# First expert product of a diffusion-transformer layer: sharing one 512-column matmul between the two halves of the activations

## The reference

```
q = (h @ w_q).reshape(B, T, PEER_HEADS, 2, PEER_DHALF)
s = einsum('bshid,hikd->bshik', q, sub_keys)
s1, i1 = top_k(s[..., 0, :], 16); s2, i2 = top_k(s[..., 1, :], 16)
top_s, pos = top_k(s1[..., :, None] + s2[..., None, :], 16)   # of the 256 sums
g = softmax(top_s)
act = gelu(einsum('cd,ced->ce', h, u[idx]))
out = einsum('ce,ced->cd', g * act, v[idx])
```

## Time and profile before

| | |
|---|---|
| median of three runs | 2128.35 us (2126.1 to 2129.22) |
| the profiled execution | 2125.87 us |
| its span, first to last instruction | 2124.1 us |
| mean granted TensorE clock | 0.993 |
| busy: PE, DVE, ACT, POOL | 2075.6, 1657.9, 1231.0, 312.1 us |
| HBM traffic | 247 GB/s over the span |

### The profile page before, as it was taken

The page is one execution under the profiler, slowest core; times in us unless marked ns, Lnnn a source line. Parts: engine busy times, 40 slices in busy tenths (PEclk is TensorE's granted clock), DMA queues, the critical chain, the costliest instruction groups (busy, mean ns, idle before and its releaser), DMA issues.

```text
span 2124.1 us, 41214 instructions
## 1 busy us (share of the span) xinstructions
PE 2075.6 (98%) x13458; PEld 1842.5 (87%) x13458; DVE 1657.9 (78%) x2947; ACT 1231.0 (58%) x2273; POOL 312.1 (15%) x264
## 2 busy tenths in 40 slices
PE   6999999999999999999999999999999999999997
PEld 3568888668999999999999999999878888888886
DVE  3467777897775688888787688888688989989997
ACT  3332225686444677777766655555566666666666
POOL 0000000000000000000000211111344555323320
PEclk9999999999999999999999999999999999999999
DMA  9968887401765455555598644445789999999992
GB/s 366 408 246 300 284 282 264 159 1 51 263 246 184 155 177 184 182 182 178 181 360 309 203 157 156 159 157 182 263 297 365 371 352 358 344 360 354 395 352 95
DMA packets 160917, 524.86 MB, mean 247 GB/s; under 512 B 34976, under 2 KB 35792, under 8 KB 160208
## 3 DMA queue, kind: packets, MB, share of 16 engines
q1 hardware_dynamic: 123840, 452.63, 59.2%
q0 software_dynamic: 20576, 67.20, 9.1%
q10 hardware_dynamic: 16432, 4.19, 0.9%
HBM read 515.52 MB, written 8.39 MB: 247 GB/s over the span
## 4 chain that ended last, share of the span: by engine, by line
PE 90%; DVE 4%; DMA 2%; ACT 2%; issue 1%; SPq 0%; POOL 0%; DVEq 0%; ACTq 0%
PE PS L890 73%; PE PS L1287 10%; PE PS L1228 2%; PE PS L946 1%; DVE st L1535 1%; DMA ada_t<-w_ada 1%; PE PS L1073 1%; DVE w_lo L1335 1%; PE PS L878 1%; PE PS L897 1%; ACT pr L634 0%; DVE mixed L1908 0%; PE PS L1061 0%; DMA x_c<-x_ctx 0%; DMA raw<-stream 0%
## 5 line engine op out<-in xcount | busy, mean ns | idle before, releaser
L475 ACT ACTIVATE w_hi<-raw 128x512 fp32r<-128x512 f32 x1088 | 682.2, 630 | 687.5 <-PE PS L890 527.5
L1335 DVE TENSOR_TENSOR w_lo<-raw,w_hi 128x512 fp32r<-128x512 f32 x1088 | 731.5, 690 | 331.0 <-ACT w_hi L475 305.2
L890 PE MATMUL PS<-h_h,w_hi 128*128 128x256 f32 (+1 forms) x2304 | 658.0, 286 | 1.6 <-ACT A L739 1.0
L890 PE MATMUL PS<-h_l,w_hi 128*128 128x256 f32 (+1 forms) x2304 | 652.8, 283 | 0.0
L890 PE MATMUL PS<-h_h,w_lo 128*128 128x256 f32 (+1 forms) x2304 | 652.8, 283 | 0.0
L890 PEld LDWEIGHTS PS<-h_h,w_hi 128*128 128x128 f32 x2304 | 443.1, 192 | 2.7 <-ACT A L739 1.2
L890 PEld LDWEIGHTS PS<-h_l,w_hi 128*128 128x128 f32 x2304 | 443.2, 192 | 0.0
L890 PEld LDWEIGHTS PS<-h_h,w_lo 128*128 128x128 f32 x2304 | 443.0, 192 | 0.0
L890 PE MATMUL PS<-w_hi,p_hl 128*128 128x512 f32 x1024 | 399.5, 390 | 6.4 <-issue 4.7
L890 PEld LDWEIGHTS PS<-w_hi,p_hl 128*128 128x128 f32 x1024 | 192.2, 188 | 50.5 <-issue 8.5
L890 PE MATMUL PS<-w_lo,p_hl 128*128 128x512 f32 x512 | 199.3, 389 | 0.0
(11 more groups left out here) (253 smaller groups left out, 2836.2 us busy)
## 6 DMA issues: line engine op xcount, KB each, us to landing
raw<-stream SPq DMA_DIRECT2D x544, 512.0 KB
raw_far<-stream SPq DMA_DIRECT2D x104, 512.0 KB
ada<-w_ada SPq DMA_DIRECT2D x96, 512.0 KB, 4.6
ada_t<-w_ada SPq DMA_DIRECT2D x64, 512.0 KB, 9.7
ada_u<-w_ada SPq DMA_DIRECT2D x32, 512.0 KB, 5.9
values_scratch<-A ACTq DMA_DIRECT2D x1, 2560.0 KB, 19.0
x_c<-x_ctx SPq DMA_DIRECT2D x1, 2048.0 KB, 7.8
x<-x_lat SPq DMA_DIRECT2D x1, 2048.0 KB, 15.2
```

What stands on the lines that cost most here:

```text
L475: nc.scalar.activation(w_hi[:, (2 * j + hf) % SPLIT, :], ring[:, j, hf * HALF:(hf + 1) * HALF], ACT.Copy).then_inc(S["w_high"], 1)
L890: ins = mm(out_, l_, r_, start=(start and q == 0), stop=(stop and q == 2), skip_group_check=check)
L1335: V_.tensor_tensor(w_lo[:, h % SPLIT, :], ring[:, h // 2 % RAW, at_:at_ + HALF], w_hi[:, h % SPLIT, :].bitcast(F32), ALU.subtract).then_in ...
```

## The change

In tiles 0 to 59, `h2_h` and `h2_l` become one tensor `h2`, and a block's products with `w_hi` are one matmul of 512 columns: `w_hi x h2_h` lands in the left half of the bank and `w_hi x h2_l` in the right. The product `w_lo x h2_h` is added to the left half. ScalarE copies the right half to SBUF (`keep_side`, into `rstd`, free by then), VectorE adds the left half to it (`sum_sides`), and gelu reads the sum from SBUF. TensorE waits for that sum (`sides_summed`) before it enters a bank again. A small gelu before each of ScalarE's loops loads the gelu table, under which Copy works too. The stretch before the gates grows by one turn (`GATES_AT` 30), with five halves in place of four at eight places of the one-hot steps. Three of POOL's six memsets move ahead of the wait for the one-column products. Tiles from 60 on are as before.

```diff
-        h2_h = at("h2_h", [P, KT, T], F32R, R + 128 * KB)
-        h2_l = at("h2_l", [P, KT, T], F32R, R + 144 * KB)
+        h2 = at("h2", [P, 2, KT, T], F32R, R + 128 * KB)
+        h2_h, h2_l = h2[:, 0], h2[:, 1]
...
+            for i in (80, 96, 104):
+                tiles_of_ones(i)
             pool.wait_ge(S["ada_col"], 8)
-            for i in range(2 * ROUTE_AT, NE_TILES, 8):
-                nc.gpsimd.memset(A[:, i:i + 8, :], 1.0).then_inc(S["tiles_one"], 1)
+            for i in (88, 112, 120):
+                tiles_of_ones(i)
...
+            def gelu_summed(i):
+                act.wait_ge(S["sides_summed"], i + 3)
+                nc.scalar.activation(A[:, bass.ds(i, 1), :].rearrange("p a t -> p (a t)"), rstd[:],
+                                     ACT.Gelu_apprx_tanh).then_inc(S["gelu_done"], 1)
+            def keep_side(i, bank):
+                act.wait_ge(S["w_free"], 4 * i + (2 * U_U + 4 + SPLIT))
+                act.wait_ge(S["gelu_done"], i + 2)
+                nc.scalar.activation(rstd[:], PS[:, bank, T:2 * T], ACT.Copy).then_inc(S["side_kept"], 1)
...
-            u_tiles(0, GATES_AT)
+            def summed_turn(b, first=False):
+                for i in range(2):
+                    split_high(b + (34 + i), (2, 0)[i])
+                    act.wait_ge(raw_in[(3, 1)[i]], 16 * b + 16 * (34 + i) + 16)
+                    half_high(b + (34 + i), (3, 1)[i], 0)
+                    if not (first and i == 0):
+                        gelu_summed(2 * b + (i - 1))
+                    keep_side(2 * b + i, i)
+                    half_high(b + (34 + i), (3, 1)[i], 1)
...
+            nc.scalar.activation(modc[:, 30:31], eps[:], ACT.Gelu_apprx_tanh)
+            summed_tiles(GATES_AT)
             act.wait_ge(S["top_s_ready"], 1)
             nc.scalar.activation(ge[:], tops[:], ACT.Exp).then_inc(S["top_exp"], 1)
+            nc.scalar.activation(modc[:, 31:32], eps[:], ACT.Gelu_apprx_tanh)
             u_tiles(GATES_AT, ROUTE_AT - GATES_AT)
...
+            def summed_product(n):
+                with pe.Fori(0, n) as b:
+                    for h in range(8):
+                        i = h // 4
+                        pe.wait_ge(S["w_low"], 8 * b + (2 * U_U + h + 1))
+                        if h % 4 == 0:
+                            pe.wait_ge(S["sides_summed"], 2 * b + (i + 1))
+                        for q in range(4):
+                            k = 4 * (h % 4) + q
+                            cols = slice(q * P, (q + 1) * P)
+                            mm(PS[:, i, :], w_hi[:, h % SPLIT, cols], h2[:, :, k, :], start=(k == 0), stop=False,
+                               skip_group_check=True)
+                            ins = mm(PS[:, i, 0:T], w_lo[:, h % SPLIT, cols], h2_h[:, k, :], start=False,
+                                     stop=(k == KT - 1), skip_group_check=True)
+                        used(ins)
...
-            first_product(0, LATE_ADA_AT + 8, False)
+            summed_product(GATES_AT)
+            first_product(GATES_AT, LATE_ADA_AT + 8 - GATES_AT, False)
...
+            def sum_sides(i):
+                dve.wait_ge(S["side_kept"], i + 1)
+                V_.tensor_tensor(rstd[:], PS[:, i % 2, 0:T], rstd[:], ALU.add).then_inc(S["sides_summed"], 1)
             half = [2 * (U_U + 2)]
             def next_low(n):
                 for _ in range(n):
+                    tile, part = divmod(half[0] - 2 * U_U, 4)
+                    if part == 3 and tile <= 2 * GATES_AT:
+                        sum_sides(tile - 1)
                     half_low(half[0] // 8, half[0] % 8)
                     half[0] += 1
...
-GATES_AT = 29
+GATES_AT = 30
```

More of the change, by code:

```diff
@@ L106, in block_program @@
                      "top_s_ready top_exp gates_ready gates_turned gates_kept gelu_done gelu_in tiles_one "
-                     "dist_b dist_b2 hot_a hot_b routed route_used p_high p_high_too p_low picks_ready picks_in far_ready values_kept mixed y_kept_a y_kept_d y_turned x3_ready x3_scaled sq_summed").split()
+                     "side_kept sides_summed dist_b dist_b2 hot_a hot_b routed route_used p_high p_high_too p_low picks_ready picks_in far_ready values_kept mixed y_kept_a y_kept_d y_turned x3_ready x3_scaled sq_summed").split()
         S = {n: ctx.enter_context(nc.semaphore(n)) for n in sem_names}
@@ L422, in _, with tiles_of_ones @@
                 nc.gpsimd.dma_start(dst[0:PICKED], near[PICKED:P, a, :]).then_inc(S["picks_in"], 16)
+            def tiles_of_ones(i):
+                nc.gpsimd.memset(A[:, i:i + 8, :], 1.0).then_inc(S["tiles_one"], 1)
+            for i in (80, 96, 104):
+                tiles_of_ones(i)
             pool.wait_ge(S["ada_col"], 8)
-            for i in range(2 * ROUTE_AT, NE_TILES, 8):
-                nc.gpsimd.memset(A[:, i:i + 8, :], 1.0).then_inc(S["tiles_one"], 1)
+            for i in (88, 112, 120):
+                tiles_of_ones(i)
             pool.wait_ge(S["gates_kept"], 6)
@@ L763, in u_tiles, with summed_tiles @@
                     gelu(2 * b + 1, 1)
-            u_tiles(0, GATES_AT)
+            def summed_turn(b, first=False):
[7 more added lines that the diff above has]
+                    half_high(b + (34 + i), (3, 1)[i], 1)
+            def summed_tiles(n):
+                summed_turn(0, first=True)
+                with act.Fori(1, n) as b:
+                    summed_turn(b)
+                gelu_summed(2 * n - 1)
+            nc.scalar.activation(modc[:, 30:31], eps[:], ACT.Gelu_apprx_tanh)
+            summed_tiles(GATES_AT)
             act.wait_ge(S["top_s_ready"], 1)
             nc.scalar.activation(ge[:], tops[:], ACT.Exp).then_inc(S["top_exp"], 1)
+            nc.scalar.activation(modc[:, 31:32], eps[:], ACT.Gelu_apprx_tanh)
             u_tiles(GATES_AT, ROUTE_AT - GATES_AT)
@@ L1247, in _ @@
             pe.sem_inc(S["gelu_done"], 2)
+            pe.sem_inc(S["sides_summed"], 2)
             pe.sem_inc(S["routed"], 2)
-            first_product(0, LATE_ADA_AT + 8, False)
+            summed_product(GATES_AT)
+            first_product(GATES_AT, LATE_ADA_AT + 8 - GATES_AT, False)
             ada_columns(6, 6, acc_u)
@@ L1780, in _ @@
                                           iota16[:].unsqueeze(1).broadcast_to([P, P, 16]), ALU.is_equal))
-                    next_low(4)
+                    next_low(5)
                     hv = hit[:].rearrange("p (h k) a -> p h k a", h=HEADS)
```

## The result

The changed kernel takes 2113.43 us (median of 7 runs, 2109.66 to 2122.25), the kernel before 2128.35 (7 runs, 2126.1 to 2131.59): ratio 0.9935, 95% interval 0.9919 to 0.9952. Twelve more runs of the same text beside 25 of the kernel before gave 2117.66 against 2127.43: ratio 0.995, 0.9934 to 0.9966. The forecast was 2116.0.

What follows compares the result with a forecast made beforehand. TensorE's matmul pitch was taken as the bound: 12.5 us saved by merged matmuls, less 0.5 at the stretch's end, gives -12.0 us, from 2128.35 to 2116.3, stated as 2116.0 us; own range 2112.5 to 2118.5, wider range 2112 to 2122.

Steps and rivals of the forecast that it cites:

- The term of 12.5 us: TensorE, tiles 0 to 59: one fixed part of 0.0130 us less per block, 60 tiles x 16 blocks, 12.5 us off.
- The forecast of 12.0: Whole kernel: 12.5 us gained in the matmuls less 0.5 lost at the end of the stretch, 12.0 us faster.
- Rival A: 512-column matmul loses its gain through its two-piece operand beside a 256; 0.2396 us or more a pair, 2129 us; chance 0.07.
- a pair above 0.35: Tiles 0 to 59: a pair step above 0.35 us would show the forecast wrong and Rival A right.
- The 333.5 us for the tiles: Sign that the forecast is right: TensorE's 60 tiles in the stretch take about 333.5 us, where they took 346.3.
- VectorE keeps up: Tiles 0 to 59: with the addition VectorE keeps up in each of three search rhythms, at 85 to 94%.
- Rival B: VectorE late at 28 wide search steps, 0.1 to 0.3 us each; 3 to 8 us, 2119 to 2124; chance 0.12.
- C's point of 0.8 us: VectorE becomes the bound if an addition with its exposed wait costs over 0.8 us; 2138 us at 1.2; chance 0.05.
- This saves nothing by itself: ScalarE, tiles 0 to 59: work falls from 4.2 to 3.3 us per tile, but TensorE never waited for it.
- case D: Table loads stay; ScalarE needs 4.6 of 5.54 us a tile and still isn't waited for; 2116 to 2118; chance 0.02.
- End of the stretch: Before the gates, TensorE's wait of 1.0 us grows as w_lo's come later; cost 0.3 to 0.6 us, 0.5 taken.

## Why the prediction was right

**The pitch.** The term of 12.5 us was 960 times the fixed part of a matmul, 13 ns, from the earlier trace rows. Measured: 0.3600 us for three of 256 (apart), 0.3467 for the pair in its fast rhythm, 13.3 ns x 960 = 12.8 us. With the fixed part of about 2.5 ns that the Trainium skill gives (TensorE: Matmul & The Clock Gate, section "Wait — 56ns, not 53.3ns?"), an estimated 960 x 2.5 ns = 2.4 us would have been gained; the runs side with the rows. That the gain is this matmul and nothing else is shown by the run with three matmuls again.

**What it had not.** The slow rhythm, 6.6 ns on 429 and 159 of the 960 pairs in the changed kernel's two traces (159 to 588 in the others with this order of matmuls and no wait in the stretch), 1 to 3 us, at most 4. With it the sum is 12.8 - 1 to 3 - 0.2 = 10 to 11.5 us; the adjusted gains are 9.8 and 10.5. The forecast of 12.0 was mis-sized by this term. Rival A had it as a price (a pair at up to 0.3594) but not as something that comes and goes: its sign, a pair above 0.35, was seen in part of each trace. The 333.5 us for the tiles were also 0.3 less than the prediction's own 346.3 - 12.5.

**VectorE keeps up.** No wait in the stretch. The addition took 421 ns (0.43 said), and it was late nowhere. The sums counted 0.43 us for it and 0.62 for a w_lo; from start to start they are 0.333 and 0.60 to 0.61, so there was more room than the sums said. Rival B did not occur; C's point of 0.8 us is bracketed by two additions (0.67 us start to start: small loss) and three (1.0: 9 us).

**ScalarE.** The copy took 385 ns, the gelu out of SBUF 402 (0.38 said). "This saves nothing by itself" holds: with three matmuls again and one table load in the stretch nothing is gained. But case D said that the loads beside the new copy would still not be waited for, and forced they cost 3.4 to 4.6 us. The step that failed there is judging it by the sum of busy times, 4.6 of 5.54 us. It bore on a rival alone.

**End of the stretch.** Waits of 0.2 + 1.0 us where 1.0 stood: +0.2, with 0.5 said. The place was right: 0.2 for a late w_lo at tile 61, then 1.0 at tile 62, which the view puts down to a gelu as it did before. The granted clock behind the one-column products was 0.84 from 1160 to 1170 us in place of 0.66, yet outside the stretch nothing was gained.

**The median.** 2116.0 was within 2.6 us of 2113.43, but in part by luck. The two medians differ by 14.9 us, more than the mechanism gives (10 to 11.5) and more than the forecast; the later runs of the same text gave 2117.66 and a difference of 9.8.

## What to carry to other kernels

Where TensorE binds, read its pitch (the time from one start to the next) for each width. If a part of it does not depend on the width, it pays to make one wide matmul of two products that share their stationary operand. The price, a copy and an addition elsewhere, is free only while those engines have room at each step. Judge that room by start-to-start times and by the one chain that the change made short, not by busy sums. With a scatter of the size of the effect, compare at equal granted clock, and beside the kernel before in the same group of runs.

## What the runs showed of the hardware

At full granted clock a stream of alternating 512- and 256-column matmuls runs at 0.3467 or at 0.3533 us a pair. Nearly always it changes between them where something breaks the stream: a wait, or a hiccup, which makes one or two steps longer, by 0.06 to 0.28 us in all. In one place, near pair 772 of the run with forced loads, it changes with no longer step beside it. The first 207 pairs have the fast rhythm in every trace without a wait there. Where nothing waits, the hiccups come after the same pairs (207, 367 or 368, 671, 831 or 832) in every trace with this order of matmuls; uniform 256-column streams have them too, at other places. Which rhythm follows is not settled by the program or the layout of the operand. A uniform stream of 256 has one rhythm (0.1200 a matmul). So has the order 512, 256, 256, 512 (0.3484 a pair), and the one grouped by four (0.3508) nearly so. What sets the rhythm stays open. With its slow pairs and its breaks added up, the length of tiles 0 to 59 comes out within 0.03 us in each of the nine traces with the alternating order.

ScalarE's loop with a Copy and a gelu in each turn has two table loads per turn when it is entered under another table (19 loads from 1060 to 1180 us without the small gelus) and none when it is entered under gelu's.
